# Expert value tiles of a decoder layer loaded in pairs of 256 rows, with expert numbers split at other bits

## The chip, the cores and the metric

The kernel runs on one core of a Trainium2 chip. The time is device microseconds (us) of one execution; the times of before are three runs, given as their median. A profile is one further execution, recorded by the hardware profiler: its own time and its span are given below. TensorE, VectorE, ScalarE, GpSimd and SyncE stand in the profile as PE, DVE, ACT, POOL and SP. DMAs run on 16 DMA engines that all queues share.

## The reference

A decoder layer with 1024 tokens of width 1024, all in float32. Three token-mixing branches (dilated attention, a gated recurrence, attention into memory) are gated and merged, a layer norm follows, and then an expert network with product keys. The change touches only the last part of the expert network:

```python
def _peer(h, w_q, sub_keys, u_tab, v_tab):            # u_tab, v_tab: 16384 experts x 1024
    ...
    s1, i1 = lax.top_k(sc[..., 0, :], PEER_TOPK)      # 16 of 128
    s2, i2 = lax.top_k(sc[..., 1, :], PEER_TOPK)
    cidx = i1 * PEER_N_KEYS + i2                      # (shown without reshapes)
    ...
    idx = jnp.take_along_axis(cidx, pos, axis=-1)     # 8 heads x 16 = 128 experts a token
    gate = jax.nn.softmax(top, axis=-1)
    def block(args):                                  # 128 tokens
        xt, it, gt = args
        act = jax.nn.gelu(jnp.einsum('td,ted->te', xt, u_tab[it]), approximate=False)
        return jnp.einsum('te,ted->td', gt * act, v_tab[it])
    ...
h = _layer_norm(DN_ALPHA * h + ffn, ln2_g[layer], ln2_b[layer])
```

So every token has 128 chosen experts, a coefficient for each (its gate times the gelu of a dot product with a row of `u_tab`), and its output is the sum of the chosen rows of `v_tab`, weighted by these coefficients.

## The kernel before

From about 1905 us on the kernel works on the expert network alone, in eight blocks of 128 tokens (n = 0 to 7). It reads the two tables in different ways.

Rows of `u_tab` are gathered. For each of a block's 128 slots k, GpSimd issues one indirect DMA (L859) that brings one row of 4 KB to each of the 128 partitions (512 KB in all) into `u_ring`, which has room for 8. VectorE takes the dot product with the tokens (L2113, `dot`), which fills column k of `coef`. Block 0's dots were made earlier, beside the projections.

Rows of `v_tab` are not gathered: the whole table is streamed through, and what a token doesn't want gets the coefficient zero. The table of 16384 rows is cut into 128 value tiles of 128 rows. A tile is 128 partitions x 1024 floats, 4 KB a partition, 512 KB in all. SyncE loads it (`load_values`, L758) into `v_ring`, which has four places. TensorE multiplies it by the coefficients (`values_of`, L1228): the left operand is `table[:, row, :]`, 128 experts x 128 tokens, the right one half of the tile's columns, and the results add up in PSUM for the whole of a block's work.

The coefficients have to be spread out into `table` first. An expert number is split into the number of its tile and its row in the tile (`split_keys`, L2086 to L2089: a shift right by 7, an and with 127, and one cast of both to float). TensorE transposes both and the coefficients (`turn`, L935), ScalarE copies them to `by_slot` (L1555), VectorE makes two 0/1 matrices for each four tokens by comparing with the numbers 0 to 127 (`hots`, L2105 and L2106), ScalarE scales one by the coefficients (L1562), TensorE multiplies the two (`pair`, L1212), which gives for each token a 128 x 128 matrix (row in the tile x tile), and ScalarE copies it into `table` (L1576).

The loop is over nine passes p = 0 to 8, each with 64 steps i. A step is one value tile. A pass streams half of the value table, and a tile serves blocks p - 1 and p, so that each block has seen the whole table after two passes. Pass 0 and pass 8 have one block each. A tile takes eight matmul instructions of the profile where it serves two blocks and four where it serves one. In the first half of a pass (steps 0 to 31) TensorE does nothing but these; VectorE does the second half of the dots of block p + 1. At step 24 VectorE does `split_keys(p + 1)`, between dots; when the last dot is in `coef`, the gelu (L1583, ScalarE) and the gates (L2118) follow. At step 30 TensorE waits for both the keys and the coefficients, for `turn(p + 1)`. In the second half (steps 32 to 63) each step has one `pair` of block p + 1 ahead of its value tile, and VectorE does two `hots` and two dots of block p + 2. In passes 0 and 1, from step 32 of the first to step 31 of the second, VectorE also picks the top experts of the last four blocks. Pass 7 has no gathers and no pairs, and pass 8 neither.

The order is written out in the code, for each engine by itself. SyncE's loads of the value tiles stand in one queue with its others: `h1` (L751), the picks (L747, L748), the residual (L791), the stores of the output (L788) and, once, `g2` and `b2` (L782, L783). Load j (j = 64 p + i) waits until tile j - 4 is used: `v_used` counts used tiles, starting at 4, and the load waits for j + 1. TensorE waits for the load by one semaphore a place, `v_in`.

## Time and profile before

| what | value |
|---|---|
| median of 3 runs | 4395.98 us (4393.19 to 4398.56) |
| the profiled execution | 4396.11 us, span 4394.3 us |
| TensorE busy, clock granted | 3776.2 us (86%), mean 0.934 |
| VectorE, GpSimd, ScalarE busy | 2632.8, 1554.4, 1265.2 us |
| DMA over the span | 1130.17 MB, mean 257 GB/s |
| loads of value tiles | 576 of 512 KB |
| gathers of `u_tab` rows in the last stage | 896 of 512 KB |

The profiled execution took 1.8 us more than its span. Shares over the whole span mix stages with different limits, so the profile is read stage by stage. The change touches the stretch from 1903 us to the end. Its passes start at 1989, 2430, 2722, 2988, 3254, 3520, 3787, 4051 and 4271 us. A name such as `v_ring<-in_peer_v` is written to from read; `coefe` is the buffer of `coef`, `h_up` that of the tokens beside the dots. In a time line, what stands in brackets is the idle time before and what ended it.

### The profile page before, as it was taken

The page shows a single profiled execution, that of the slowest core. Times are in us where ns is not written, and L with a number is a line of the kernel's source. Part 1 is how long each engine was busy: PE and PEld are TensorE (multiplying, and loading weights), DVE is VectorE, ACT ScalarE, POOL GpSimd, SP SyncE. Part 2 cuts the span into 40 slices and gives each one's busy share as a digit, 9 for nine tenths or more (in the row PEclk, how much of TensorE's full clock was granted, in tenths as well). Part 3 has the DMA queues.
Part 4 walks back from the last instruction along what each step waited for, and adds up shares of the span by engine and source line. Part 5 has one row for each costly group of instructions (what it writes and reads, how often), then busy time and mean ns, then how long its engine had stood idle before and what let it go on. Part 6 is the DMA issues. An engine that isn't in the chain of part 4 may idle for free.

```text
span 4394.3 us, 45248 instructions
## 1 busy us (share of the span) xinstructions
PE 3776.2 (86%) x14175; PEld 2439.4 (56%) x14175; DVE 2632.8 (60%) x5301; ACT 1265.2 (29%) x2545; POOL 1554.4 (35%) x1317
## 2 busy tenths in 40 slices
PE   7999889799899797665265969899898998989998
PEld 5777777677777676552133435354454544445443
DVE  1544443227777665576999988686776868742000
ACT  1444433224434432260033023041331404224000
POOL 2555444220000476555322344444444444410000
PEclk9999999899999999878677989999999999999999
DMA  7666523364454478689766899999999999963457
GB/s 244 202 204 201 191 79 95 95 206 131 129 159 146 146 246 285 217 307 381 269 223 225 323 364 382 396 373 401 379 382 385 374 409 363 389 260 125 158 171 274
DMA packets 503228, 1130.17 MB, mean 257 GB/s; under 512 B 37836, under 2 KB 249980, under 8 KB 502688
## 3 DMA queue, kind: packets, MB, share of 16 engines
q1 hardware_dynamic: 345248, 575.67, 38.4%
q0 software_dynamic: 147456, 536.94, 33.0%
q10 hardware_dynamic: 10368, 15.73, 1.0%
q8 instruction: 68, 1.11, 0.1%
q14 instruction: 88, 0.72, 0.0%
HBM read 1041.14 MB, written 89.41 MB: 257 GB/s over the span
## 4 chain that ended last, share of the span: by engine, by line
PE 27%; DMA 13%; DVE 12%; issue 3%; POOL 1%; DVEq 0%; ACT 0%
PE ps L1228 23%; DMA u_ring<-in_peer_u,pidx 12%; DVE u_ring L2113 5%; PE ps L1212 4%; POOL u_ring L859 1%; DMA v_ring<-in_peer_v 1%; DVE hot L2105 1%; DVE hot L2106 1%; DVE pick_own L1753 0%; DVE pick_own L1758 0%; DVE got_own L1761 0%; DVE inds_own L1716 0%; DVE inds_own L1704 0%; DVE left_own L1707 0%; PE h_up L1201 0%
## 5 line engine op out<-in xcount | busy, mean ns | idle before, releaser
L1228 PE MATMUL ps<-v_ring,table 128*128 128x512 f32 x4096 | 1841.0, 603 | 21.4 <-DMA v_ring<-in_peer_v 19.9
L1228 PEld LDWEIGHTS ps<-v_ring,table 128*128 128x128 f32 x4096 | 773.5, 194 | 917.3 <-issue 864.5
L859 POOL DMA_INDIRECT u_ring<-in_peer_u,pidx x896 | 861.9, 962 | 1134.6 <-DVE coefe L2113 1064.1
L2113 DVE CUSTOM_DVE_ANT_0 u_ring<-u_ring,h_up 128x1024 f32<-128x1024 f32 x896 | 1067.4, 1218 | 234.5 <-DMA u_ring<-in_peer_u,pidx 210.2
L808 POOL TENSOR_TENSOR w_lo<-w_raw,w_hi 128x1024 fp32r<-128x1024 f32 x200 | 445.9, 2236 | 885.3 <-ACT w_hi L1301 880.0
L918 PE MATMUL ps<-x_hi,w_hi 128*128 128x512 f32 x1280 | 519.5, 406 | 64.2 <-ACT w_hi L1301 55.7
L921 PE MATMUL ps<-x_lo,w_hi 128*128 128x512 f32 x1280 | 506.6, 396 | 0.0
L1212 PEld LDWEIGHTS ps<-hot,hot 128*128 128x128 f32 x2048 | 294.3, 211 | 245.5 <-DVE hot L2106 136.0
L1212 PE MATMUL ps<-hot,hot 128*128 128x128 f32 x2048 | 309.0, 300 | 120.1 <-DVE hot L2106 96.5
L1562 ACT ACTIVATE hot<-hot,by_slot 128x128 f32<-128x128 f32 x1024 | 321.1, 389 | 189.9 <-DVE hot L2105 185.9
L1576 ACT ACTIVATE table<-ps 128x512 f32<-128x512 f32 (+3 forms) x256 | 229.0, 895 | 448.5 <-PE ps L1212 284.5
L918 PEld LDWEIGHTS ps<-x_hi,w_hi 128*128 128x128 f32 x1280 | 245.9, 192 | 130.6 <-ACT w_hi L1301 37.6
L927 PE MATMUL ps<-x_hi,w_lo 128*128 128x512 f32 x1280 | 316.3, 389 | 0.0
L2105 DVE TENSOR_TENSOR hot<-keys,by_slot 128x512 f32<-128x512 f32 x256 | 177.3, 692 | 228.3 <-PE ps L1212 167.7
L921 PEld LDWEIGHTS ps<-x_lo,w_hi 128*128 128x128 f32 x1280 | 245.6, 192 | 51.7 <-issue 1.9
L927 PEld LDWEIGHTS ps<-x_hi,w_lo 128*128 128x128 f32 x1280 | 240.2, 188 | 49.9
L1791 DVE CUSTOM_DVE_ANT_0 e_ring<-e_ring,h_up 128x1024 f32<-128x1024 f32 x128 | 155.7, 1221 | 157.9 <-DMA e_ring<-in_peer_u,icole 138.4
L2126 DVE SCALAR_TENSOR_TENSOR res<-res,ps 128x512 f32<-128x512 f32 x16 | 10.3, 684 | 346.8 <-PE ps L1228 346.8
L1583 ACT ACTIVATE coefe<-coefe 128x128 f32<-128x128 f32 x7 | 2.2, 311 | 748.7 <-DVE coefe L2113 716.3
L816 POOL TENSOR_TENSOR w_hi<-w_raw,zero 128x1024 fp32r<-128x1024 f32 x56 | 109.7, 1958 | 259.0 <-PE ps L918 122.8
L2106 DVE TENSOR_TENSOR hot<-keys,by_slot 128x512 f32<-128x512 f32 x256 | 175.7, 686 | 0.0
L1301 ACT ACTIVATE w_hi<-w_raw 128x1024 fp32r<-128x1024 f32 (+1 forms) x144 | 132.1, 917 | 149.2 <-DMA w_raw<-in_w_branch 47.7
(288 smaller groups left out, 3882.8 us busy)
## 6 DMA issues: line engine op xcount, KB each, us to landing
v_ring<-in_peer_v SPq DMA_DIRECT2D x576, 512.0 KB
w_raw<-in_w_in SPq DMA_DIRECT2D x104, 512.0 KB
wh_d<-w_hi SPq DMA_DIRECT2D x56, 512.0 KB, 2.7
wl_d<-w_lo SPq DMA_DIRECT2D x56, 512.0 KB, 4.2
w_hi<-wh_d SPq DMA_DIRECT2D x56, 512.0 KB, 3.6
w_lo<-wl_d SPq DMA_DIRECT2D x56, 512.0 KB, 3.8
w_raw<-in_w_peer_q SPq DMA_DIRECT2D x32, 512.0 KB
u_ring<-in_peer_u,pidx POOLq DMA_INDIRECT x896
```

Source lines behind the costliest of these rows:

```text
L808: pool.tensor_tensor(out=w_lo[b][:, 0:k, :], in0=w_raw[b][:, 0:k, :], in1=w_hi[b][:, 0:k, :].bitcast(F32), op=ALU.subtract).then_inc(w_spl ...
L859: pool.indirect_dma_start(out=u_ring[:, k % U_ROWS, :], out_offset=None, in_=u_tab, in_offset=bass.IndirectOffsetOnAxis(ap=pidx[n % 2][:, ...
L918: first = pe.matmul(out, w_hi[b][:, k, :], hi[:, k, :], start=(k == 0), stop=False)
L921: pe.matmul(out, w_hi[b][:, k, :], lo[:, k, :], start=False, stop=False)
L927: last = pe.matmul(out, w_lo[b][:, k, :], hi[:, k, :], start=False, stop=(k == k_n - 1))
L1212: last = pe.matmul(build_bank(item)[:, P * m:P * m + P], hot2[sub % 2][:, m, :], hot1[sub % 2][:, m, :], start=True, stop=True)
L1228: last = pe.matmul(ps[2 * (n % 2) + c][:, :], table[:, row_of(n, i1), :], v_ring[:, j % V_TILES, HALF * c:HALF * c + HALF], start=(n == p ...
L1562: last = act.activation(hot1[sub % 2][:, m, :], hot1[sub % 2][:, m, :], ACT.Copy, scale=by_slot[:, 2, t0 + m:t0 + m + 1])
L1576: last = act.activation(table[:, r0:r0 + near, t0:t0 + TOK].rearrange("p i t -> p t i"), src[:, :, 0:near], ACT.Copy)
L2105: dve.tensor_tensor(out=hot1[sub % 2][:, :, :], in0=numbers(NTILE * (n % 2)), in1=of(0), op=ALU.is_equal).then_inc(hot_one, 1)
L2106: dve.tensor_tensor(out=hot2[sub % 2][:, :, :], in0=numbers(0), in1=of(1), op=ALU.is_equal).then_inc(hot_ready, 1)
L2113: dve.tensor_tensor_reduce(out=u_ring[:, k % U_ROWS, :], in0=u_ring[:, k % U_ROWS, :], in1=h1_up[:, :, :].rearrange("p c n -> p (c n)"), s ...
```

## The change

An expert number e is taken apart at other bits. Before, the tile was e >> 7 and the row e & 127. Now the tile is 2 (e >> 8) + (e & 1) and the row is (e >> 1) & 127. So the even and the odd rows of 256 neighbouring rows make two tiles, and on each partition the two rows of a pair of tiles lie next to each other in memory, 8 KB in one piece. One DMA loads the pair (1024 KB) into two neighbouring places of `v_ring`. The ring keeps its 16 KB a partition, but as two pairs. A load is issued at even steps only, and it waits until both tiles of the pair that had its place are used: until tile j - 3 is used. There are two semaphores `v_in` in place of four; TensorE waits for the pair's at each tile. VectorE splits the keys with five operations in place of three: the tile number is put together from its upper bits, cast, and its lowest bit, added afterwards, with a wait on VectorE's own semaphore ahead of the third, fourth and fifth.

```diff
--- before.py
+++ after.py
@@ -454,7 +454,7 @@
         h1_in, h1_raised = sem("h1_in"), sem("h1_raised")
         res2_in = sem("res2_in")
         u_in = [sem(f"u_in{i}") for i in range(U_ROWS)]
-        v_in = [sem(f"v_in{i}") for i in range(V_TILES)]
+        v_in = [sem(f"v_in{i}") for i in range(V_TILES // 2)]
         v_used = sem("v_used")
         u_dots, u_gelu, u_coef = sem("u_dots"), sem("u_gelu"), sem("u_coef")
         key_split, key_ready = sem("key_split"), sem("key_ready")
@@ -753,9 +753,9 @@
             def load_values(p, i):
 
                 j = NTILE * p + i
-                first = P * tile_key(p, i)
-                sp.wait_ge(v_used, j + 1)
-                sp.dma_start(v_ring[:, j % V_TILES, :], v_tab[first:first + P, :]).then_inc(v_in[j % V_TILES], 16)
+                first, slot = P * tile_key(p, i), j % V_TILES
+                sp.wait_ge(v_used, j + 2)
+                sp.dma_start(v_ring[:, slot:slot + 2, :], v_tab[first:first + 2 * P, :].rearrange("(p b) d -> p b d", b=2)).then_inc(v_in[slot // 2], 16)
 
             load_picks(0)
             load_picks(1)
@@ -789,7 +789,8 @@
                     if i == 44 and p >= 2:
                         sp.wait_ge(p_out, 16 * (p - 1))
                         sp.dma_start(res2[:, :], h1_d[p - 1]).then_inc(res2_in, 16)
-                    load_values(p, i)
+                    if i % 2 == 0:
+                        load_values(p, i)
             sp.wait_ge(FV.sem, FV.after("sb", NBLK - 1))
             sp.dma_start(out_d[0, P * (NBLK - 1):P * NBLK, :], res2[:, :]).then_inc(p_out, 16)
             sp.wait_ge(p_out, 16 * NBLK)
@@ -1216,7 +1217,7 @@
 
                 j = NTILE * p + i
                 i1 = tile_key(p, i)
-                pe.wait_ge(v_in[j % V_TILES], 16 * (j // V_TILES) + 16)
+                pe.wait_ge(v_in[j % V_TILES // 2], 16 * (j // V_TILES) + 16)
                 for n in range(max(p - 1, 0), min(p, NBLK - 1) + 1):
                     if n == p and i == 0:
                         pe.wait_ge(build_out, pair_item(p, NSUB - 1) + 1)
@@ -2083,10 +2084,14 @@
                 if n:
                     dve.wait_ge(turned, n)
                     dve.wait_ge(paired, NSUB * n)
-                dve.tensor_scalar(out=key_u[:, 0, :], in0=pidx[n % 2][:, :], scalar1=7, scalar2=None, op0=ALU.logical_shift_right)
-                dve.tensor_scalar(out=key_u[:, 1, :], in0=pidx[n % 2][:, :], scalar1=P - 1, scalar2=None, op0=ALU.bitwise_and).then_inc(key_split, 1)
-                dve.wait_ge(key_split, n + 1)
-                dve.tensor_copy(key_f[:, :, :], key_u[:, :, :]).then_inc(key_ready, 1)
+                dve.tensor_scalar(out=key_u[:, 0, :], in0=pidx[n % 2][:, :], scalar1=7, scalar2=2 * P - 2, op0=ALU.logical_shift_right, op1=ALU.bitwise_and)
+                dve.tensor_scalar(out=key_u[:, 1, :], in0=pidx[n % 2][:, :], scalar1=1, scalar2=P - 1, op0=ALU.logical_shift_right, op1=ALU.bitwise_and).then_inc(key_split, 1)
+                dve.wait_ge(key_split, 3 * n + 1)
+                dve.tensor_copy(key_f[:, :, :], key_u[:, :, :]).then_inc(key_split, 1)
+                dve.wait_ge(key_split, 3 * n + 2)
+                dve.tensor_scalar(out=key_u[:, 0, :], in0=pidx[n % 2][:, :], scalar1=1, scalar2=None, op0=ALU.bitwise_and).then_inc(key_split, 1)
+                dve.wait_ge(key_split, 3 * n + 3)
+                dve.tensor_tensor(out=key_f[:, 0, :], in0=key_f[:, 0, :], in1=key_u[:, 0, :], op=ALU.add).then_inc(key_ready, 1)
 
             def hots(n, sub):
 
```

SyncE's order, its last rows (pass 6 from step 44, pass 7 and pass 8; `out` and `res` are the output's store and the residual's load), first of before:

```order
L791 DMA res_170<-h_d 128x1024 [waits p_out]
L758 DMA v_ring<-in_peer_v 128x1024 [waits v_used] x44
L788 DMA out<-res_170 128x1024 [waits fin_dve]
L758 DMA v_ring<-in_peer_v 128x1024 [waits v_used] x20
L791 DMA res_170<-h_d 128x1024 [waits p_out]
L758 DMA v_ring<-in_peer_v 128x1024 [waits v_used] x20
```

And the same place of after:

```order
L791 DMA res_170<-h_d 128x1024 [waits p_out]
L758 DMA v_ring<-in_peer_v 128x2048 [waits v_used] x22
L788 DMA out<-res_170 128x1024 [waits fin_dve]
L758 DMA v_ring<-in_peer_v 128x2048 [waits v_used] x10
L791 DMA res_170<-h_d 128x1024 [waits p_out]
L758 DMA v_ring<-in_peer_v 128x2048 [waits v_used] x10
```

Half as many loads of twice the size; what stands between them stays between the same steps.

SyncE's order in pass 1 about step 48, where `h1` (`h`), `g2`, `b2` and the picks are loaded (before):

```order
L758 DMA v_ring<-in_peer_v 128x1024 [waits v_used] x39
L751 DMA h_169<-h_d 128x1024 [waits h1_raised]
L782 DMA g_171<-in_ln_g 128x1024 [waits tk_out]
L783 DMA b_172<-in_ln_b 128x1024
L747 DMA pidx_173<-idx_d 128x128 [waits turned]
L748 DMA pgate_175<-gate_d 128x128
L758 DMA v_ring<-in_peer_v 128x1024 [waits v_used] x40
```

After:

```order
L758 DMA v_ring<-in_peer_v 128x2048 [waits v_used] x19
L751 DMA h_169<-h_d 128x1024 [waits h1_raised]
L782 DMA g_171<-in_ln_g 128x1024 [waits tk_out]
L783 DMA b_172<-in_ln_b 128x1024
L747 DMA pidx_173<-idx_d 128x128 [waits turned]
L748 DMA pgate_175<-gate_d 128x128
L758 DMA v_ring<-in_peer_v 128x2048 [waits v_used] x20
```

The five loads stand between steps 47 and 48 in both. The load ahead of them is now that of steps 46 and 47 together, and the one behind them that of 48 and 49.

VectorE's order at `split_keys` of the last block (pass 6, step 24), before:

```order
L2113 ISA u_ring,coefe<-u_ring,h_up 128x1024 [waits u_in1]
L2113 ISA coefe 128x1
L2086 TENSOR_SCALAR key_u<-pidx_174 128x128 [waits paired,turned,pk_in1]
L2087 TENSOR_SCALAR key_u<-pidx_174 128x128
L2089 CAST key_f<-key_u 128x256 [waits key_split]
L2113 ISA u_ring,coefe<-u_ring,h_up 128x1024 [waits u_in2]
```

After (the dot is L2118 there):

```order
L2118 ISA u_ring,coefe<-u_ring,h_up 128x1024 [waits u_in1]
L2118 ISA coefe 128x1
L2087 TENSOR_SCALAR key_u<-pidx_174 128x128 [waits paired,turned,pk_in1]
L2088 TENSOR_SCALAR key_u<-pidx_174 128x128
L2090 CAST key_f<-key_u 128x256 [waits key_split]
L2092 TENSOR_SCALAR key_u<-pidx_174 128x128 [waits key_split]
L2094 TENSOR_TENSOR key_f<-key_f,key_u 128x128 [waits key_split]
L2118 ISA u_ring,coefe<-u_ring,h_up 128x1024 [waits u_in2]
```

Two operations of 128 x 128 are added at the same place between two dots.

## Rows read from the trace of the kernel before

**Rows 1.** The page, part 2: tenths busy in 40 slices of 110 us.

```profile
PE   7999889799899797665265969899898998989998
...
DMA  7666523364454478689766899999999999963457
```

**Rows 2.** The chain of waits in pass 3: start us, us, what.

```profile
3026.44 14.42 DMA u_ring<-in_peer_u,pidx
...
3093.61 10.23 issue
...
3108.12 7.37 PE ps L1228 x16
```

**Rows 3.** Time line of TensorE, `turn` of pass 3.

```profile
3103.83 0.66 PE L935 MATMUL ps<-ident,key_f 128*128 128x128 f32 x2 [12.98 <-issue]
```

**Rows 4.** Busy us by stretch: PE, PEld, DVE, ACT, POOL; TensorE's clock, DMA share, GB/s.

```profile
1992.00:2046.00 54.00, 40.95 (x97) 15.70 (x95) 31.04 (x52) 0.00 (x0) 24.47 (x27) 0.99 1.02 401
2987.70:3093.00 105.30, 103.15 (x241) 45.40 (x239) 70.79 (x119) 1.49 (x2) 52.71 (x54) 1.00 1.02 409
3093.00:3116.20 23.20, 12.37 (x31) 6.20 (x32) 15.38 (x28) 3.37 (x10) 10.44 (x11) 0.71 0.95 363
3116.20:3253.80 137.60, 137.60 (x507) 76.38 (x506) 112.21 (x189) 66.58 (x153) 59.34 (x63) 1.00 0.99 371
4051.20:4270.90 219.70, 219.70 (x513) 97.25 (x512) 6.33 (x11) 0.20 (x1) 0.00 (x0) 1.00 0.48 158
4270.90:4384.90 114.00, 111.76 (x257) 47.61 (x255) 5.46 (x9) 0.20 (x1) 0.00 (x0) 1.00 0.85 290
```

**Rows 5.** The chain of waits in pass 8.

```profile
4288.26 5.18 DMA v_ring<-in_peer_v
...
4307.93 6.30 DMA v_ring<-in_peer_v
...
4349.51 34.79 PE ps L1228 x80
```

**Rows 6.** The DMA view, 3010 to 3070 us.

```profile
DMA packets 6742, 24.60 MB, mean 410 GB/s; under 512 B 742, under 2 KB 742, under 8 KB 6740
```

**Rows 7.** The DMA view, 68.6 to 70.4 us, pieces of 8 KB only.

```profile
DMA packets 95, 0.78 MB, mean 432 GB/s; under 512 B 0, under 2 KB 0, under 8 KB 0
```

**Rows 8.** Time line of VectorE at `split_keys` of pass 3.

```profile
3093.05 0.22 DVE L2087 TENSOR_SCALAR key_u<-pidx 128x128 uint32<-128x128 uint32 x1
3093.30 0.29 DVE L2089 CAST key_f<-key_u 128x256 f32<-128x256 uint32 x1
3094.17 1.22 DVE L2113 CUSTOM_DVE_ANT_0 u_ring<-u_ring,h_up 128x1024 f32<-128x1024 f32 x1 [0.58 <-DMA u_ring<-in_peer_u,pidx]
```

**Rows 9.** Time line of SyncE, two loads in pass 7 (start us, us).

```profile
4202.43 3.76 SPq L758 DMA_DIRECT2D v_ring<-in_peer_v  x2
```

**Rows 10.** The DMA view, 4202.2 to 4205.6 us; tenths busy in 40 slices.

```profile
DMA  0000000000000193447534999599998967323100
...
DMA packets 144, 0.52 MB, mean 154 GB/s; under 512 B 16, under 2 KB 16, under 8 KB 144
```

**Rows 11.** The DMA view's issues: KB each, median us to landing.

```profile
w_hi<-wh_d SPq DMA_DIRECT2D x56, 512.0 KB, 3.6
...
mem_n<-in_mem SPq DMA_DIRECT2D x1, 1024.0 KB, 9.1
...
h1e<-h_d SPq DMA_DIRECT2D x1, 512.0 KB, 3.3
```

**Rows 12.** Time line of TensorE, start of pass 0.

```profile
2004.88 1.98 PE L1228 MATMUL ps<-v_ring,table 128*128 128x512 f32 x4 [0.69 <-DMA v_ring<-in_peer_v]
2007.44 1.98 PE L1228 MATMUL ps<-v_ring,table 128*128 128x512 f32 x4 [0.58 <-DMA v_ring<-in_peer_v]
```

**Rows 13.** The chain of waits about step 48 of pass 1.

```profile
2636.99 16.29 DMA v_ring<-in_peer_v
```

**Rows 14.** Time line of TensorE at step 48 of pass 1.

```profile
2653.33 3.70 PE L1228 MATMUL ps<-v_ring,table 128*128 128x512 f32 x8 [2.50 <-DMA v_ring<-in_peer_v]
```

## The prediction

> **What bounds the kernel now.** The page's second part comes first: from slice 24 to 35 (some 2600 to 3900 us) TensorE's line and that of the DMA engines are both at 8 or 9 tenths [rows 1], so it can't say which of the two sets the time. The stretches are therefore read one by one. In pass 3, which stands for passes 2 to 6 (each takes 105.3 + 23.2 + 137.6 = 266.1 us), the chain of waits runs in the first half through the gathers, pieces such as 14.42 us for eight rows, then over VectorE's last dots (the 10.23 us "issue" behind the key split) to TensorE at 3103.83 [rows 2]. TensorE had been idle for 12.98 us by then [rows 3]. So TensorE has 13 us to spare in the first half of each such pass, and the DMA engines have nothing: share 1.02, 409 GB/s [rows 4]. In the second half TensorE is busy for all of 137.60 us [rows 4], 4.30 us a step, and nothing is to spare there. Pass 7 is 219.70 us of matmul without a pause, 3.43 us a step, the DMA engines half idle (0.48) [rows 4]. Pass 8 has one block a tile, so 1.72 us a step, 109.9 us for 64; it took 114.0 [rows 4], and the chain goes several times over a load of a value tile, 5.18 and 6.30 us from issue to use [rows 5]. There, four loads in flight are just enough.
>
> In short: the gathers' bandwidth bounds the first halves, TensorE the second ones and pass 7, and pass 8 stands on the edge between TensorE and the latency of a load.
>
> **What the larger pieces give.** In a gathering stretch 24.60 MB went in 60 us, 410 GB/s, in pieces of 4 KB but for the small ones [rows 6]; a pair of tiles (1.05 MB) costs 2.56 us of all engines. Where only 8 KB pieces ran, a store early in the kernel, it was 432 GB/s [rows 7], by which a pair costs 2.43 us. This bounds the gain at 0.13 us a pair; the lower bound is nothing. About 17 pairs are loaded in the gathering half of a pass (16 for its steps and what the ring takes in ahead): 2.2 us at most. I take 1.5, since rows 7 is a store with nothing beside it. Passes 0 and 2 to 6, and the end of pass 1's first half, wait so: six times 1.5 is 9 us. In the second halves and pass 7 a quicker transfer gives nothing, since TensorE is the bound.
>
> **What the longer key split costs.** One more operation like L2087 (0.22 us) and one addition of about the same size, each with a wait: some 0.5 us between two dots in the gather-bound part. The dots behind it had waited 0.58 us for their row [rows 8], so that it may cost nothing; at worst it is 0.5 us x 6. I charge the 3 us. Gain and this cost leave -6 us.
>
> **What the ring of two pairs costs.** Before, a load is issued when tile j - 4 is used, and three tiles are still to be worked on. Now a pair's load is issued when the pair before the last is used, and only one pair, two tiles, is left to work on, while twice the bytes have to land. Cover is 2 x 4.30 = 8.6 us in the second halves, 6.87 us in the first halves and in pass 7, and 3.43 us in pass 8.
>
> How long does a pair's load take from the last matmul that frees its place to the first that uses it? A lone 512 KB load in pass 7 was issued at 4202.43 [rows 9]; its packets lie in slices 14 to 38 of 40, from 4203.3 to 4205.4 [rows 10], the last 3.0 us after the issue. From issue to landing such loads take 3.3 us (`h1e`) and 3.6 us (`w_hi`, the median of 56) [rows 11]. Another 512 KB at 410 GB/s is 1.28 us. That makes 4.6 to 4.9, and I take 4.9, as SyncE's and TensorE's start have to be in it as well. The bounds from both sides: 3.9, if the whole megabyte flowed at 432 GB/s (2.43 us) between the 0.9 us before the first packet and some 0.5 behind the last; and 9.1, the one 1024 KB load for which the view has a time [rows 11]. That one ran at the start of the kernel among many others, so I weigh it little; nearer is 5.18 + 1.28 = 6.5, from a tile's load in pass 8 with others in flight [rows 5].
>
> Pass 8: the load of a pair is issued as TensorE begins the pair before it (3.43 us). The first comes 4.9 - 3.43 = 1.47 us late; the next was issued 3.43 us after it and is then just in time; the third is late again. So 16 of the 32 pairs wait for 1.47 us, 23.5 us in all. Against this stand the 4.1 us that pass 8 loses now (114.0 - 109.9), which are of the same kind. With some 0.6 us for the residual's load and the store in the same queue, pass 8 becomes 20 us longer. At 3.9 us a load it is +3.4, at 6.5 us +45.
>
> Passes 0 to 6, beside the gathers: in pass 0 TensorE waited for each tile, one every 2.56 us [rows 12], 205 GB/s, while both queues together moved 401 [rows 4]: the two queues then share the engines half and half, packet by packet. If an 8 KB piece counts as one packet, a pair's queue gets two thirds, 273 GB/s: 3.84 us for the pair in place of 2.56 alone, thus 4.9 + 1.28 = 6.2 us; if the engines share by bytes, 7.5 us. Cover of 8.6 us in the second halves holds against both. Cover of 6.87 us in the first halves holds against the first; against the second it misses (7.5 - 6.87)/2 = 0.3 us a pair, 5 us a half, which the idle 13 us take up. The price in passes 2 to 6 is nothing. Pass 7, with no gathers, has 6.87 against 4.9: nothing.
>
> The Trainium skill (DMA: Bandwidth & Descriptors, Queues, rings and completion order) says that each DMA engine takes turns between its queues packet by packet; the trace agrees, by the 2.56 us. By this rule larger packets would take bandwidth from the gathers, which are the bound of the first halves. It changes no term, because the value tiles' bytes are the same and their queue falls idle the sooner.
>
> Step 48 of pass 1: here `h1`, `g2`, `b2` and the picks stand between the loads of two steps, and the load behind them took 16.29 us [rows 13], of which TensorE waited for 2.50 [rows 14]. Now the pair ahead of them and the pair behind them bring 512 KB more each: 2 x 1.28 = 2.6 us later at two thirds of the bandwidth, 5.1 at a half. TensorE is the bound there, so I add 2.5 us. The order of SyncE's other DMAs stays, and the load of the queries in passes 0 and 1 is asked for several steps ahead.
>
> **The sum.** -6 for the pieces and keys, +20 for pass 8, +2.5 for pass 1: +16.5. On the profiled execution's 4396.1 us (span 4394.3, 1.8 around it, 0.1 from the median of 3 runs) this gives 4412.6; I say 4412. Forecast's own range: 4402 to 4424.
>
> **Rivals.**
>
> *Faster.* A pair's load in pass 8 takes no more than 3.9 us, because large pieces flow at the full rate even alone. Then pass 8 loses 16 x 0.47 = 7.5, 3.4 more than now, the gathering halves give the whole 2.2 us six times (-13), the key split hides and so does pass 1: 4396.1 - 10 = 4386. For it: rows 7, 432 GB/s in 8 KB pieces. Against it: the lone load of rows 10, whose engines started raggedly and moved 0.52 MB in 2.1 us. It decides from a load of 4.3 us down. The Trainium skill (DMA: Bandwidth & Descriptors, Rules for kernel authors) asks for 1 MiB or more a DMA, which is what is done here; it would make this rival the likeliest. The fit that the Trainium skill gives there (Anatomy of one DMA), 2.0 us and bytes over 436 GB/s, gives 4.4 us for this load, by which pass 8 would be 11 us longer. No row here shows a lone load of 1 MiB from the value table.
>
> *No change.* Loads of 4.4 us, halfway from the bound of 3.9 to my 4.9, cost pass 8 11.4 us net, the full -13 is had, and pass 1 costs 2.5: 4397.
>
> *Slower still, by waits in all passes.* A load beside the gathers takes over 8.6 us from free to used. Then the second halves, where nothing is to spare, lose (L - 8.6)/2 a pair: at 9.1 us [rows 11] 0.25 x 16 x 6 = 24 us, and pass 8 with 6.5 us costs 45 in place of 20: 4396.1 + 45 + 24 - 6 + 2.5 = 4462; with the 45 alone 4438. Against it: the pieces of pass 0's waits above give 7.5 us at most.
>
> *The loads remain in 4 KB pieces*, two a partition. Nothing is gained, the split costs 3, and the ring costs what it costs: 4396.1 + 3 + 20 + 2.5 = 4422. The page's count of packets under 8 KB would tell.
>
> *TensorE's clock falls in pass 8.* In pass 0, at 1992 to 2046 us, TensorE was busy for 40.95 of 54 us in steps of 1.98 us with pauses of 0.6, and the granted clock was 0.99 [rows 4, 12]; in pass 8 it would pause for 1.5 of 8.3 us. I give it nothing of its own.
>
> **Chances.** Forecast 0.55, waits everywhere or long loads 0.13, 4 KB pieces 0.06, no change 0.15, faster 0.11. What a measurement here can tell from no change is about 0.2%, 9 us. Slower: 0.55 + 0.13 + 0.06 = 0.74; same 0.15; faster 0.11. The range takes in the no-change case down to 4395 and the dearer loads up to 4432 (a load of 6 us in pass 8); beyond it lie the faster case and most of the third rival.
>
> **What would show it.** Pass 8 (from the last waiting of pass 7 to the end of the matmuls) takes 134 us in place of 114, with a wait of about 1.5 us before every second pair; the load to its use is 4.9 us. Pass 7 stays at 219.7. Passes 2 to 6 take 265 in place of 266.1, all of the difference in the first half. The wait at step 48 of pass 1 is 5 us. 73728 packets of 4 KB become 36864 of 8 KB. I am wrong if pass 8 stays under 120 us, or if waits for `v_ring` stand in the second halves.

## The result

| what | before | changed kernel |
|---|---|---|
| median of 7 runs | 4395.98 us (4388.41 to 4401.56) | 4415.39 us (4410.05 to 4427.03) |
| ratio to before | | 1.0046, 95% interval 1.0032 to 1.0060 |
| span of the profiled execution | 4394.3 us | 4413.6 us |

The changed kernel is 0.46% slower. It was forecast at 4412 us, slower, between 4395 and 4432.

The spans differ by 19.3 us. By the first matmuls of the passes (the starts of before stand above; those of after are 1991.4, 2430.0, 2730.4, 2994.4, 3259.4, 3521.1, 3782.6, 4043.0 and 4262.7) it divides so:

| stretch | before | after | change | forecast |
|---|---|---|---|---|
| ahead of pass 0, and pass 0 | 2430.3 | 2430.0 | -0.3 | -1 |
| pass 1 | 291.5 | 300.4 | +8.9 | +2.5 |
| passes 2 to 6 | 1329.4 | 1312.6 | -16.8 | -5 |
| pass 7 | 219.7 | 219.7 | 0 | 0 |
| pass 8, to the last matmul | 113.2 | 140.6 | +27.4 | +20 |

(The forecast of -6 for larger pieces and keys is spread here over pass 0 and passes 2 to 6, 1 us each.) Pass 1, passes 2 to 6 and pass 8 each moved the way they were forecast, and each by more: 13.8 us too much on the slower side, 11.8 on the faster. That the sum came out within 4 us of the measured median is in part luck, since the errors cancelled.

The page after, from its second and third part. Columns as before; the last line counts packets by size.

```profile
PEclk8999999899999899877677989999999999999999
DMA  7666523364444478689666899999999999953456
...
DMA packets 461754, 1130.14 MB, mean 256 GB/s; under 512 B 33228, under 2 KB 245372, under 8 KB 424352
```

Before, 502688 of 503228 packets were under 8 KB, now 424352 of 461754: 36864 pieces of 8 KB took the place of 73728 of 4 KB, as the change says (the page shows 36862 more packets of 8 KB and over than before).

The stretches after (pass 1 in two halves, passes 2 to 6, pass 7, pass 8), with the columns of [rows 4]:

```profile
2430.00:2583.10 153.10, 118.45 (x298) 53.62 (x297) 141.37 (x386) 4.95 (x12) 65.72 (x70) 0.90 0.93 349
2583.10:2730.40 147.30, 140.65 (x507) 77.23 (x505) 113.33 (x191) 66.35 (x153) 59.20 (x63) 0.98 0.93 349
2730.40:4043.00 1312.60, 1266.88 (x3872) 630.36 (x3872) 914.70 (x1545) 355.98 (x889) 539.10 (x565) 1.00 0.92 360
4043.00:4262.70 219.70, 219.70 (x513) 97.28 (x512) 6.32 (x11) 0.20 (x1) 0.00 (x0) 1.00 0.44 158
4262.70:4403.30 140.60, 117.21 (x257) 46.79 (x255) 4.91 (x8) 0.20 (x1) 0.00 (x0) 0.99 0.66 239
```

And passes 2 to 6 of before:

```profile
2721.80:4051.20 1329.40, 1262.98 (x3873) 638.79 (x3872) 915.34 (x1537) 356.95 (x889) 540.82 (x565) 0.97 0.93 356
```

Look at the clock, 0.97 before and 1.00 after, and at pass 8's GB/s, 290 before [rows 4] and 239 after.

The chain of waits in the first half of pass 4, which answers to [rows 2]:

```profile
3266.47 7.09 DMA v_ring<-in_peer_v
...
3288.74 9.31 DMA v_ring<-in_peer_v
...
3335.64 8.12 DMA v_ring<-in_peer_v
...
3359.88 14.00 PE ps L1229 x32
3373.88 0.33 PE ps L936 x3
3374.21 1.72 PE h_up L1202 x4
3375.93 6.87 PE ps L1229 x16
```

The chain no longer goes through gathers. It goes over the loads of the value tiles (six of them in this half, 7.09 to 9.31 us from issue to use) and TensorE. The turn follows without a wait, and raising `h1` takes 1.72 us where it took 3.41 before.

The turn needs the coefficients too, and the time lines show which of the two came last. Before, in pass 4 (it starts at 3253.8), the coefficients were ready at 3370.0 and TensorE turned at once; in the changed kernel (pass 4 starts at 3259.4) they were ready at 3370.1 and TensorE turned at 3373.7:

```profile
3369.74 0.29 DVE L2118 TENSOR_TENSOR coefe<-coefe,pgate 128x128 f32<-128x128 f32 x1 [0.38 <-issue]
3370.13 0.66 PE L935 MATMUL ps<-ident,key_f 128*128 128x128 f32 x2 [13.20 <-issue]
```

```profile
3369.80 0.29 DVE L2123 TENSOR_TENSOR coefe<-coefe,pgate 128x128 f32<-128x128 f32 x1 [0.38 <-ACT coefe L1584]
3373.72 0.38 PE L936 MATMUL ps<-ident,key_f 128*128 128x128 f32 x2
```

So the gathers ended 5.5 us sooner after the pass's start, and TensorE, held up by its own tiles, was 3.6 us later than they. It is TensorE that bounds the first half there. The DMA engines are as full as they were [rows 4]:

```profile
3259.40:3375.80 116.40, 107.24 (x249) 45.85 (x248) 80.20 (x138) 2.59 (x5) 58.85 (x61) 1.00 1.02 412
```

Pass 8, two pairs of the chain, which answers to [rows 5]:

```profile
4360.89 4.78 DMA v_ring<-in_peer_v
4365.67 0.04 issue
4365.72 3.71 PE ps L1229 x8
4369.43 0.02 issue
4369.45 4.78 DMA v_ring<-in_peer_v
```

A load is issued, used 4.78 + 0.04 us later, TensorE works for 3.71 us, and the next load of the chain is issued at once: 8.56 us for two pairs, where the matmuls of these four tiles at full pace would be 6.87.

### The profile page after: what moved, and what is told of

It reads as the page before. It is cut to its first block, busy times and chain, and to the rows that moved or that the text cites. A ratio compares the mean times of both kernels' runs of the same rounds, so it can differ in the third digit from the quotient of the medians.

```text
span 4413.6 us, 44976 instructions
## 1 busy us (share of the span) xinstructions
PE 3798.7 (86%) x14175; PEld 2435.4 (55%) x14175; DVE 2632.1 (60%) x5317; ACT 1262.7 (29%) x2545; POOL 1550.3 (35%) x1317
## 2 busy tenths in 40 slices
DMA packets 461754, 1130.14 MB, mean 256 GB/s; under 512 B 33228, under 2 KB 245372, under 8 KB 424352
## 4 chain that ended last, share of the span: by engine, by line
PE 33%; DVE 11%; DMA 11%; issue 2%; POOL 0%; DVEq 0%; SPq 0%; ACT 0%
PE ps L1229 29%; DMA v_ring<-in_peer_v 8%; DVE u_ring L2118 4%; PE ps L1213 4%; DMA u_ring<-in_peer_u,pidx 3%; DVE hot L2111 1%; DVE hot L2110 1%; DVE pick_own L1754 0%; DVE pick_own L1759 0%; DVE got_own L1762 0%; DVE inds_own L1717 0%; DVE inds_own L1705 0%; DVE left_own L1708 0%; DVE pos_own L1743 0%; DVE pos_own L1732 0%
## 5 line engine op out<-in xcount | busy, mean ns | idle before, releaser
L1229 PE MATMUL ps<-v_ring,table 128*128 128x512 f32 x4096 | 1871.8, 608 | 108.3 <-DMA v_ring<-in_peer_v 105.6
L2118 DVE CUSTOM_DVE_ANT_0 u_ring<-u_ring,h_up 128x1024 f32<-128x1024 f32 x896 | 1064.2, 1216 | 202.6 <-DMA u_ring<-in_peer_u,pidx 193.7
```

The lines of the kernel that those rows point to most:

```text
L1229: last = pe.matmul(ps[2 * (n % 2) + c][:, :], table[:, row_of(n, i1), :], v_ring[:, j % V_TILES, HALF * c:HALF * c + HALF], start=(n == p ...
L2118: dve.tensor_tensor_reduce(out=u_ring[:, k % U_ROWS, :], in0=u_ring[:, k % U_ROWS, :], in1=h1_up[:, :, :].rearrange("p c n -> p (c n)"), s ...
```

## The experiments

A word on how they are read. The first matmul of pass 0 came at 1984 to 1999 us in the profiles below, though the kernels hardly differ ahead of it, and single runs of the kernel before lay between 4388 and 4413 us. The medians tell a few tenths of a per cent; the passes tell more, since pass 7 took 219.7 us in each profile. So each experiment is judged by its passes first. Pass 1 is less steady: it took 291.6, 293.7 and 295.8 us in three kernels (e10, e8, e7) of which the last two change nothing in it, so that 2 to 4 us there mean little.

| kernel | median us | ratio to before (95%) | pass 1 | passes 2 to 6 | pass 8 |
|---|---|---|---|---|---|
| before | | 1 | 291.5 | 1329.4 | 113.2 |
| changed | 4415.39 | 1.0046 (1.0032 to 1.0060) | 300.4 | 1312.6 | 140.6 |
| e1, new split, single loads | 4408.61 | 1.0019 (1.0005 to 1.0033) | 293.4 | 1329.4 | 121.0 |
| e2, pairs in 4 KB pieces | 4468.02 | 1.0176 (1.0158 to 1.0194) | 300.8 | 1365.3 | 138.9 |
| e3, pass 8 in single loads | 4399.80 | 0.9999 (0.9985 to 1.0014) | 298.2 | 1309.1 | 122.0 |
| e4, TensorE paced | 4386.67 | 0.9967 (0.9957 to 0.9978) | 303.3 | 1306.6 | 113.5 |
| e5, tiles loaded later | 4378.07 | 0.9959 (0.9945 to 0.9974) | 292.6 | 1309.4 | 113.3 |
| e7, paced from pass 2 | 4375.83 | 0.9943 (0.9929 to 0.9956) | 295.8 | 1304.3 | 114.2 |
| e8, paced and later | 4369.76 | 0.9946 (0.9931 to 0.9961) | 293.7 | 1302.8 | 113.8 |
| e9, ring of three pairs | 4406.70 | 1.0018 (1.0009 to 1.0028) | 291.3 | 1339.4 | 110.1 |
| e10, busy before the turn, 26 | 4398.07 | 0.9999 (0.9989 to 1.0009) | 291.6 | 1329.4 | 112.6 |
| e11, three pairs, paced, later | 4380.90 | 0.9961 (0.9948 to 0.9975) | 292.8 | 1309.0 | 109.9 |
| e12, busy before the turn, 56 | 4396.11 | 0.9996 (0.9983 to 1.0009) | 297.4 | 1319.2 | 115.3 |

### e1: the key split alone

```diff
+sp.wait_ge(v_used, j + 1)          # P * (tile_key(p, i) // 2 * 2) is first
+sp.dma_start(v_ring[:, slot, :], v_tab[first:first + 2 * P, :].rearrange("(p b) d -> p b d", b=2)[:, i % 2, :]).then_inc(v_in[slot], 16)
```

> The new key split alone: expert numbers are taken apart as in the changed kernel, but each tile is loaded by itself (every other row of 256, 4 KB pieces), ring of four tiles, as before. My theory (the price lies in the lead of the ring, the gain in TensorE coming late to the turn): all passes as before, passes 2 to 6 at 266 us, pass 8 at 113 to 114, pass 1 at 291 to 293, the two added VectorE operations cost 0 to 3 us in all; 4396 to 4399 us. Rival (the new split itself costs or gains): 4390 or less, or 4403 or more, spread over passes 1 to 6.

Measured, passes 2 to 6 and pass 8 (columns as in [rows 4]):

```profile
2730.70:4060.00 1329.30, 1260.94 (x3872) 638.15 (x3871) 917.63 (x1547) 356.03 (x889) 541.02 (x565) 0.97 0.92 356
4279.80:4401.20 121.40, 114.83 (x257) 46.70 (x255) 5.05 (x9) 0.20 (x1) 0.00 (x0) 1.00 0.79 272
```

Passes 2 to 6 stand at 1329.3 us, as before: the two operations added on VectorE cost nothing there. In the changed kernel they take 0.23 and 0.29 us, and the dot behind them still waits for its row, which answers to [rows 8]:

```profile
3358.33 0.23 DVE L2092 TENSOR_SCALAR key_u<-pidx 128x128 uint32<-128x128 uint32 x1
3358.59 0.29 DVE L2094 TENSOR_TENSOR key_f<-key_f,key_u 128x128 f32<-128x128 f32 x1
3359.30 1.22 DVE L2118 CUSTOM_DVE_ANT_0 u_ring<-u_ring,h_up 128x1024 f32<-128x1024 f32 x1 [0.41 <-DMA u_ring<-in_peer_u,pidx]
```

The median of 4408.61 us missed the expected 4396 to 4399. The miss is pass 8, 121 us and not 113. A tile whose rows are every other one of 256 is slower to load than one of 128 neighbours: in pass 7, where each load is alone, the last packet came 3.3 us after the issue by the median, in place of 2.9. With 1.9 us more in pass 1, these 7.8 us and a start of pass 0 7 us later than in the profile of before make up the time; the last of these is no effect of the split that a row shows.

### e2: the pairs and the short ring, without the 8 KB pieces

```diff
+sp.wait_ge(v_used, j + 2)          # keys as before, first = P * tile_key(p, i)
+sp.dma_start(v_ring[:, slot:slot + 2, :], v_tab[first:first + 2 * P, :].rearrange("(b p) d -> p b d", b=2)).then_inc(v_in[slot // 2], 16)
```

> Pair loads and the ring of two pairs alone: the keys are split as before, and one DMA brings two tiles of neighbouring numbers, each partition's rows in two pieces of 4 KB. My theory: as the changed kernel within 5 us, 4410 to 4420; pass 8 at 140 to 144 us, passes 2 to 6 at 260 to 265 us in place of 266, since neither comes from the size of the pieces. Rival (8 KB pieces give the gain of passes 2 to 6, as I had it in the prediction): passes 2 to 6 at 266 us, total 4428 to 4434.

```profile
2721.30:4086.60 1365.30, 1280.53 (x3871) 635.51 (x3872) 911.70 (x1535) 355.89 (x889) 539.43 (x565) 0.99 0.90 346
4306.40:4445.50 139.10, 116.75 (x257) 46.18 (x255) 4.92 (x9) 0.20 (x1) 0.00 (x0) 1.00 0.69 241
```

Neither theory said this: 4410 to 4420 us, or 4428 to 4434, were expected, and 4468 came. Pass 8 is as in the changed kernel, so its price lies with the pairs and the ring, not with the pieces. But passes 2 to 6 take 52.7 us more than in the changed kernel.

The two kernels have the same ring, the same lead and the same bytes; e1 has shown that the key split costs these passes nothing. What is left is the size of the pieces, and with it where they lie (one of 8 KB, or two of 4 KB that are 128 rows apart). Alone, in pass 7, a pair's load landed after 4.8 us by the median in both forms (e2, and e3, whose passes up to 7 are the changed kernel's). Beside the gathers' 4 KB packets, in the first halves of passes 2 to 6, it landed after 8.0 us in 8 KB pieces (e3) and after 9.3 in 4 KB pieces (8.9 to 10.5 on the chain of pass 3). So the pieces matter where two queues compete. From 3010 to 3070 us the queue of the value tiles (packets, MB, share of the engines) had, in the changed kernel and in e2:

```profile
q1 hardware_dynamic: 1108, 8.16, 32.8%
```

```profile
q1 hardware_dynamic: 1836, 7.06, 29.4%
```

TensorE's waits for tiles in passes 2 to 6 (us in total, times, longest), first of the changed kernel:

```profile
PE ps L1229 <- DMA v_ring<-in_peer_v: 45.3, 44, 2.3
```

```profile
PE ps L1229 <- DMA v_ring<-in_peer_v: 85.8, 54, 3.2
```

With the slower first matmuls behind a wait and some half clock, the turn comes 19 to 24 us a pass later here than 30 steps at full pace (103.1 us), and 11 to 15 there. The gathers end sooner in e2 than in any other kernel, and TensorE turns only 14 to 20 us behind them. The Trainium skill (DMA: Bandwidth & Descriptors, Queues, rings and completion order) has each engine take turns between queues by the packet; that a queue with larger packets gets more of the engines agrees with it. The Trainium skill's packet is a run of several descriptors, though, and no row shows that it is what the profile counts as one.

### e3: pass 8 back to single loads

```diff
+if p == NBLK:                      # first is that of the pair
+    sp.wait_ge(v_used, j + 1)
+    sp.dma_start(v_ring[:, slot, :], v_tab[first:first + 2 * P, :].rearrange("(p b) d -> p b d", b=2)[:, i % 2, :]).then_inc(v_one[slot], 16)
```

> The changed kernel, but in pass 8 each tile is loaded by itself (every other row of 256, 4 KB pieces), as soon as its own place is free. My theory: pass 8 falls from 140.7 to 113 to 115 us, the rest stays: 4386 to 4390 us, faster than both kernels. Rival (pass 8's price is in the strided reading or in the DMA engines, not in the lead of one pair): pass 8 stays over 125 us.

```profile
2734.80:4043.90 1309.10, 1264.02 (x3872) 629.33 (x3873) 914.93 (x1545) 355.97 (x889) 540.38 (x565) 1.00 0.92 361
4263.60:4386.00 122.40, 115.26 (x257) 46.65 (x255) 5.04 (x9) 0.20 (x1) 0.00 (x0) 1.00 0.78 270
```

18.6 of the 27.4 us come back, and the 9 that don't are those of e1, the reading of every other row. So the lead of the ring is most of pass 8's price. The whole is no faster than before: its span is 1.5 us over before's, with a start of pass 0 that is 8 us later. The expectation of 4386 to 4390 us fell by the 9 us and by that start.

### e4 and e7: TensorE held to the dots, nothing else changed

```diff
 pe.wait_ge(v_in[j % V_TILES], 16 * (j // V_TILES) + 16)
+if 2 <= p + 1 < NBLK and 3 <= i < TURN_TILE:       # e7: 3 <= p + 1
+    pe.wait_ge(u_dots, dots_before(p + 1, dots_by(p + 1, i - 3)) + U_ROWS)
```

> The kernel before, with TensorE held back in the first halves of passes 1 to 6: at step i from 3 to 29 it also waits until the dots that VectorE does up to step i - 3 are done. Loads, keys and ring are those of before. My theory (passes 2 to 6 gained because TensorE's idle time of 13 us before the turn was spread out: fewer value tiles are loaded ahead of the last gathers, 1 MB or 2.3 us, and the granted clock doesn't fall to half behind it, another 2.3 us): passes 2 to 6 at 260 to 263 us, wait before the turn under 5 us, clock 1.00 there; total 4370 to 4380. Rival (the gain is of the DMA pieces): passes 2 to 6 at 266 us or more, total 4396 or more.

e4, pass 1 and passes 2 to 6:

```profile
2439.10:2742.40 303.30, 269.93 (x802) 132.71 (x801) 252.88 (x573) 71.29 (x165) 124.78 (x133) 0.95 0.93 344
2742.40:4049.00 1306.60, 1266.09 (x3873) 630.50 (x3872) 915.59 (x1537) 356.01 (x889) 540.84 (x565) 1.00 0.94 362
```

Passes 2 to 6 fall by 22.8 us with the old loads, keys and ring. So TensorE's waits spread out before the turn are enough for a gain of the changed kernel's size (16.8 us), whatever spreads them; how its gain divides is read below. Pass 1, where VectorE's top-k sets the pace, became 12 us longer, which the expectation (4370 to 4380 us) had left out and which kept the median at 4386.67. So the hold was left out there:

> As the paced kernel (TensorE of the kernel before held to the dots), but in passes 2 to 6 only; in pass 1, where VectorE's top-k sets the pace, the hold had cost 10 us. Pass 1 back at 291 to 293, passes 2 to 6 at 260 to 263 us; total 4373 to 4380 against 4398 of before: faster than both kernels. If the hold's effect in pass 1 was by chance: pass 1 stays at 300.

```profile
2725.60:4029.90 1304.30, 1266.30 (x3872) 631.79 (x3871) 915.07 (x1537) 355.72 (x889) 538.93 (x565) 1.00 0.94 363
```

Passes 2 to 6 are as expected; pass 1 came down to 295.8, not wholly to 291.5. At 0.9943 (0.9929 to 0.9956) it is faster than both kernels.

### e5, e10 and e12: bytes or clock

```diff
 sp.wait_ge(v_used, j + 1)
+if i == TURN_TILE + 1 and 2 <= p + 1 < NBLK:       # e5
+    sp.wait_ge(u_dots, dots_before(p + 2, 0) + U_ROWS)
```

> The kernel before, but in passes 1 to 6 SyncE loads tile 31 and those behind it only when all dots of block p + 1 are done, so that 3 tiles (1.6 MB) no longer go ahead of the last gathers. TensorE still idles for over 10 us before the turn. It tells the two parts of the gain apart. Bytes count: passes 2 to 6 lose about 3 x 1.28 = 3.8 us less what the clock keeps, 262 to 263 us, with 10 us and more of half clock still there; total 4375 to 4382. If it is the clock alone: 266 us, total 4396 to 4400.

```profile
2720.90:4030.30 1309.40, 1262.45 (x3872) 638.83 (x3871) 913.49 (x1537) 355.85 (x889) 539.34 (x565) 0.98 0.94 362
```

20.0 us less, 4.0 a pass, at a clock of 0.98, and the median is as expected: the three tiles that were no longer loaded ahead of the last gathers are worth 3.8 us by the bytes. TensorE still idled before each turn, 46.9 us in the five passes.

```diff
 if i == TURN_TILE and p + 1 < NBLK:
     ...
+    if p >= 1:                                     # e12: range(56)
+        pe.wait_ge(build_out, turn_item(p + 1) - 1)
+        for r in range(26):
+            pe.matmul(build_bank(turn_item(p + 1))[:, 0:P], ident[:, :], ident[:, :], start=True, stop=True)
     turn(p + 1)
```

> The kernel before, and TensorE multiplies the identity with itself 26 times (some 12 us, results not used) before the turns of passes 1 to 6, in place of idling there; loads and bytes are unchanged. It isolates the clock. If the half clock behind the idle time costs what the rows say (transposes, raising h1 and two tiles, 2.7 us), the clock stays 1.00 and passes 2 to 6 take 263 to 264 us, total 4382 to 4386. If the clock costs nothing: 266 us, 4397.

Time line of TensorE in e10, pass 4 (the products, the turn, raising `h1`):

```profile
3356.73 5.97 PE L1253 MATMUL ps<-ident 128*128 128x128 f32 x52
3371.44 0.66 PE L935 MATMUL ps<-ident,key_f 128*128 128x128 f32 x2 [8.74 <-issue]
...
3372.11 3.17 PE L1201 MATMUL h_up<-h,ident 128*128 128x512 f32 x4
```

The 26 products took 5.97 us, not 12, and TensorE idled for 8.74 us behind them; raising `h1` took 3.17 us, at the half clock for the most part. It doesn't separate the two, as the clock was at half at the turn again. With enough of the products:

> As e10, with 56 products of the identity (26 took only 5.8 us and left 8.7 us of idle time, half clock still there at the turn): 56 take 12.5 us and fill the idle time. If the half clock behind it costs what the rows say: the transposes and raising h1 at full clock (0.33 and 1.72 us in place of 0.87 and 3.41), two tiles in 6.87 us, passes 2 to 6 at 263 to 264.5 us, their sum 10 us less. If the clock costs nothing: their sum is 1329 us again.

```profile
3361.26 12.67 PE L1253 MATMUL ps<-ident 128*128 128x128 f32 x112
3375.81 0.41 PE L935 MATMUL ps<-ident,key_f 128*128 128x128 f32 x2 [1.88 <-issue]
...
3376.16 1.88 PE L1201 MATMUL h_up<-h,ident 128*128 128x512 f32 x4
```

And passes 2 to 6 of e12:

```profile
2730.40:4049.60 1319.20, 1313.54 (x4432) 696.75 (x4431) 915.12 (x1537) 355.95 (x889) 540.94 (x565) 1.00 0.93 359
```

Now the clock is 1.00, raising `h1` takes 1.88 us, and the passes are 10.2 us shorter, with every byte loaded as before. (Pass 1 took 6 us more, so that the whole gains nothing.)

How much is clock and how much is not can be read in the traces, by cutting each pass at its turn. The sums over passes 2 to 6, in us: from the first value matmul of the pass until the coefficients are ready, from there until the turn's first matmul, and from the turn to the end of the pass.

| kernel | to the coefficients | from them to the turn | from the turn on |
|---|---|---|---|
| before | 581.7 | 0.5 | 747.2 |
| changed | 553.9 | 23.6 | 735.1 |
| e2 | 534.6 | 88.8 | 742.0 |
| e4 | 570.8 | 0.5 | 735.3 |
| e5 | 562.3 | 0.5 | 746.6 |
| e7 | 568.6 | 0.5 | 735.3 |
| e9 (below) | 592.0 | 0.5 | 746.8 |
| e12 | 583.5 | 0.5 | 735.3 |

The last column is the clock's: 12 us less, 2.4 a pass, in e12, which changes nothing else, and the same in the changed kernel, e4 and e7. So the half clock behind the idle time was worth 12.1 of the changed kernel's 16.8 us. (e12 as a whole gained less, since its turns came 0.4 us a pass later, for which no row gives a reason.) The first column is the gathers': e5, which only puts tiles off, takes 19.4 us off it. In the changed kernel the gathers end 27.8 us sooner in all, and 23.1 of these go in the second column, in TensorE's wait for its own tiles. The 4.7 us that are left fit tiles asked for later as well as the 1% of bandwidth below; no run separates the two.

### e9: three pairs in the ring

```diff
-U_ROWS = 8
-V_TILES = 4
+U_ROWS = 6
+V_TILES = 6
```

(The gathers' places are counted through all blocks, as 128 is no multiple of 6.)

> The changed kernel with a ring of three pairs in place of two; to make room, the ring of gathered rows has 6 places in place of 8. Pass 8 has no gathers, so it reads the lead alone: cover 6.87 us against 4.8 us a load, 110 to 113 us in place of 140.7. In passes 2 to 6 the value tiles are again far ahead: TensorE idles before the turn, half clock 10 us and more, 265 to 268 us a pass (8 KB pieces give 0.5 to 1 us, six rows in flight may cost some). Rival (8 KB pieces themselves gave the gain of passes 2 to 6): 260 to 262 us a pass.

Passes 2 to 6 and pass 8, and the DMA view of 60 us in pass 3, which answers to [rows 6]:

```profile
2728.50:4067.90 1339.40, 1262.67 (x3873) 638.82 (x3872) 918.45 (x1547) 356.01 (x889) 541.57 (x567) 0.97 0.91 354
4287.60:4397.80 110.20, 110.20 (x257) 48.36 (x255) 4.89 (x8) 0.20 (x1) 0.00 (x0) 1.00 0.82 295
```

```profile
DMA packets 5581, 24.83 MB, mean 414 GB/s; under 512 B 626, under 2 KB 626, under 8 KB 4478
```

Pass 8 has no wait left: 110.1 us, 30.5 less than in the changed kernel. So its whole price is the lead. Pass 1's is gone as well (291.3 us). In passes 2 to 6 TensorE is early again, the clock is 0.97 again and the gain is gone. The 8 KB pieces moved 414 GB/s there in place of 410: the gain of bandwidth is 1%, some 1.1 us in a first half of 116. The passes are 10 us longer than before's, all of it ahead of the turn. One more pair loaded ahead of the last gathers would cost 2.6 us a pass by the bytes, which is enough; six rows in flight in place of eight may have a part, and the two are not separated.

### e8 and e11: the best of it together

```diff
 # e8: the kernel before with e7's wait of TensorE, and in load_values
+if i == TURN_TILE + 1 and 3 <= p + 1 < NBLK:
+    sp.wait_ge(u_dots, dots_before(p + 2, 0) + U_ROWS)
 # e11: e9's kernel with e7's wait of TensorE, and the same line with TURN_TILE + 2
```

> Both edits in passes 2 to 6: TensorE paced by the dots, and tiles 31 and later loaded after the last dot. In the paced kernel fewer bytes are left to put off (16.7 MB of tiles before the turn in place of 17.2). If bytes and clock add up: passes 2 to 6 at 257 to 260 us, total 4363 to 4372. If the loads now come too late for tiles 30 to 33: waits behind the turn, 262 us or more.

```profile
2719.70:4022.50 1302.80, 1265.23 (x3873) 630.01 (x3872) 915.61 (x1537) 355.76 (x889) 539.17 (x565) 1.00 0.94 363
```

26.6 us less than before in passes 2 to 6, 1.5 less than e7: pacing has most of it already, and the expected 257 to 260 us a pass were not reached. By the medians e8 is the fastest kernel here, by the intervals no different from e7, and some 1% faster than the changed kernel.

> The changed kernel with three pairs and six gathered rows, TensorE paced by the dots and tiles 32 and later loaded after the last dot, both in passes 2 to 6. If the parts add up: pass 1 at 291, passes 2 to 6 at 261 to 264 us (the six rows cost some of the 26 us), pass 8 at 110: 4366 to 4378, faster than both kernels and about as fast as the paced kernel with later loads. If six rows in flight cost more with TensorE paced: passes 2 to 6 at 266 or more.

```profile
2730.10:4039.10 1309.00, 1266.18 (x3872) 633.46 (x3871) 918.01 (x1547) 356.00 (x889) 543.29 (x567) 0.99 0.93 362
```

The passes are as expected, pass 8 at 109.9 among them. The median of 4380.90 us is over the expected 4366 to 4378, and the whole (0.9961) doesn't beat e7 or e8.

## Why the prediction was right, and where it was not

**The ring of two pairs in pass 8: right in mechanism and nearly in size.** 16 pairs of 32 were to wait for 1.47 us; the chain shows a period of 8.56 us for two pairs, 1.69 over 6.87. The load was 4.78 us from issue to landing, and 4.9 was taken for that and the starts on both sides. TensorE's waits were as forecast, 16 of them and 23.4 us in all. What had been left out is that the first eight matmuls behind a wait take 3.71 us, not 3.43. 16 x 1.69 is 27 us. The store and the residual's load add 1.4 (chain pieces of 5.97 and 4.97 us in place of 4.78), where 0.6 was taken; a load of 5.46 us, for which no row gives a reason, adds 0.7, and one stretch of 3.4 us at half clock 1.7. The 3.3 us that pass 8 lost before go off. That makes 27.5, where 27.4 were measured and 20 forecast. e9 shows the whole of it to be the lead.

**Step 48 of pass 1: the term of 2.5 us was mis-sized.** The wait was to be 5 us and was 5.66. But it didn't end there: the granted clock was at half behind it.

```profile
2658.21 6.29 PE L1229 MATMUL ps<-v_ring,table 128*128 128x512 f32 x8 [5.66 <-DMA v_ring<-in_peer_v]
```

```profile
2656.60:2663.40 6.80, 5.19 (x6) 2.18 (x7) 0.00 (x0) 0.00 (x0) 0.86 (x1) 0.50 0.99 402
```

The eight matmuls took 6.29 us where they took 3.70 before [rows 14]. Wait and clock together make 3.2 + 2.6 of the 7.0 us that the second half of pass 1 became longer; one more wait of 1.0 us, ahead of pass 2's first tile, is most of the rest.

**The larger pieces and the waits in the first halves: the step that failed.** The prediction had the pieces give 1.5 us a pass by bandwidth, up to 2.2, and priced TensorE's waits at nothing. The bandwidth was near: 414 GB/s in place of 410, some 1.1 us a pass. (The nine us for it count six stretches, while the prediction names seven.) But the passes gained 3.4 us each, 2.4 of them by the clock, which had no term. I had the load of a pair beside the gathers at 6.2 us, or 7.5 if the engines shared by bytes, and called 0 to 5 us of waits a half harmless, since 13 us were idle. The loads on the chain were 7.1 to 9.3 us, and the waits were 9.1 us a half by the view and 11 to 15 with what they bring behind them. They do not fit the time that was free: with the gathers sooner done, that was 8 us and not 13, and TensorE came 3.6 to 7.1 us behind the coefficients. That a gain was left is luck; in e2, where the waits are longer, there is none. The prediction had the queues' share of the engines change no term; with the larger pieces taken back, passes 2 to 6 took 52.7 us more (e2). And "the idle time takes them up" was only half of the account: idle time in one piece ahead of the turn had its own price, the half clock behind it, and spreading it gave that back. It was there to be read before: the clock of 0.71 in the third line of [rows 4].

**The longer key split: 3 us charged, nothing measured** in passes 2 to 6 (e1), by the cover that was named.

**The rivals.** Loads stayed in one piece (the packets say so). The clock fell in pass 8 for 3.4 us only. Waits in the second halves of passes 2 to 6 did not come, 137.6 us in each; in e2 they do, 4.6 us in all. The faster case asked for a load of 4.3 us or less in pass 8; it was 4.8. The Trainium skill's rule of 1 MiB or more a DMA (DMA: Bandwidth & Descriptors, Rules for kernel authors), which spoke for it, is one for bandwidth; such loads gave 1% of it here, and cost time where the ring holds only two of them. The Trainium skill's fit (Anatomy of one DMA), 2.0 us and bytes over 436 GB/s, was made for DMAs that GpSimd issues. As an estimate for SyncE's it gives 4.4 us; measured were 4.8 to the landing.

## What to carry to other kernels

Size a ring by its lead: from the moment a place is freed to its use, the work still to be done must be longer than a load of that size. Making loads larger in the same room cuts the lead and lengthens the load, and is paid in the stage that does least work a byte. Idle time that is harmless for an engine off the path may still have a price: what it let run ahead takes the bandwidth of the stream that is the bound, and TensorE came back from it at half clock. Holding a fast engine to the pace of the slow stream, by a wait or two on its counter, gave 0.5% here with the same bytes. And time that is free beside a stream is free only as long as the stream: when the change lets the stream end sooner, the engine beside it may become the bound.

## What the runs showed of the hardware that was not expected

- Beside a stream of 4 KB packets on another queue, a 1 MB load landed after 8.0 us in 8 KB pieces (e3) and after 9.3 us in 4 KB pieces (e2), by the median over the first halves of passes 2 to 6; alone, in pass 7, after 4.8 us in both. The engines moved 414 and 410 GB/s from 3010 to 3070 us (changed kernel and e2).
- Tiles made of every other 4 KB row took 0.4 us longer to load alone than tiles of neighbouring rows, and pass 8 was 8 us longer for it (e1).
- TensorE's clock was at half (1.2 of 2.4 GHz) for 13.7 us of each of passes 2 to 6 before, in and behind 13 us of idle time, and never where these were filled with spare products (e12). With waits of up to 2.3 us (changed kernel) it was at half for 3.4 us in two of the passes and not in the others, with waits of up to 3.2 us (e2) for 0 to 13.7 us a pass. In pass 8 it stayed at 1.00 in e2, with 18 waits of up to 1.9 us, and fell to half for 3.4 us in the changed kernel, behind a wait of 2.6.
